# Triangular inverse in the delta-rule mixer: 64x64 diagonal blocks throughout, or 32x32 blocks for the first four levels

## What is computed

```
m = jnp.where(strict, jnp.einsum("bhnid,bhnjd->bhnij", k_beta, k) * decay, 0.0)
a_mat = jnp.eye(CHUNK, dtype=q.dtype) + m
u = lax.linalg.triangular_solve(a_mat, v_beta, left_side=True, lower=True)
w = lax.linalg.triangular_solve(a_mat, k_beta * jnp.exp(g)[..., None], left_side=True, lower=True)
```

## Time and profile before

| | |
|---|---|
| median of 3 runs | 1297.12 us (1296.31 to 1297.67) |
| the profiled execution, its own time | 1297.02 us |
| its span | 1295.2 us |
| PE busy | 1258.4 us, 97% of the span |
| VectorE busy | 994.9 us, 77% |
| ScalarE busy | 685.0 us, 53% |
| GpSimd busy | 53.7 us, 4% |
| chain that ended last | PE 73%, VectorE 6%, DMA 2% |

### The profile page before, as it was taken

How to read it: one execution, slowest core, us unless ns; L and a number is a source line. 1 busy time by engine, 2 the same in 40 slices (tenths; PEclk the granted TensorE clock), 3 DMA queues, 4 the chain that set the end, 5 groups by cost and what they waited for, 6 DMA issues and landing times.

```text
span 1295.2 us, 29136 instructions
## 1 busy us (share of the span) xinstructions
PE 1258.4 (97%) x10579; PEld 1210.5 (93%) x10579; DVE 994.9 (77%) x1817; ACT 685.0 (53%) x1116; POOL 53.7 (4%) x93
## 2 busy tenths in 40 slices
PE   9999998999999999999999999999999999999997
PEld 8989898999999899999998899998899999999986
DVE  6897748998878898998877787775566668777654
ACT  6865435655543544665553555554365565645541
POOL 0002000000001000000000000000000000000000
PEclk9999999999999999999999999999999999999999
DMA  7550123588888588388875366665455335666651
GB/s 269 160 150 2 52 82 115 199 301 278 294 281 278 200 291 270 113 305 278 276 252 167 98 198 184 186 197 192 135 179 180 125 106 178 189 184 179 227 177 34
DMA packets 64778, 244.74 MB, mean 189 GB/s; under 512 B 7200, under 2 KB 8512, under 8 KB 64704
## 3 DMA queue, kind: packets, MB, share of 16 engines
q1 hardware_dynamic: 54048, 204.77, 48.7%
q0 software_dynamic: 10656, 38.93, 9.5%
HBM read 242.63 MB, written 1.05 MB: 188 GB/s over the span
## 4 chain that ended last, share of the span: by engine, by line
PE 73%; DVE 6%; DMA 2%; issue 1%; ACT 1%; DVEq 0%; POOLq 0%; ACTq 0%
PE ps L1778 17%; PE ps L1779 17%; PE ps L1780 16%; PE ps L2137 9%; PE ps L2138 5%; DMA ring<-in_ada_w 2%; DVE wlo L410 1%; PE ps L1793 1%; PE ps L1799 1%; PE ps L1794 1%; DVE ring L1298 1%; PE ps L2282 1%; PE ps L2284 1%; PE ps L2283 1%; DVE xb L1423 1%
## 5 line engine op out<-in xcount | busy, mean ns | idle before, releaser
L1778 PE MATMUL ps<-hhi,whi 128*128 128x258 f32 (+4 forms) x1952 | 557.6, 286 | 5.0 <-DVE hlo L1038 1.9
L1779 PE MATMUL ps<-hlo,whi 128*128 128x258 f32 (+4 forms) x1952 | 553.8, 284 | 0.0
L1780 PE MATMUL ps<-hhi,wlo 128*128 128x258 f32 (+4 forms) x1952 | 553.3, 283 | 0.0
L403 ACT ACTIVATE whi<-raw 128x1024 fp32r<-128x1024 f32 (+1 forms) x360 | 399.9, 1113 | 285.2 <-PE ps L1780 166.3
L410 DVE TENSOR_TENSOR wlo<-raw,whi 128x1024 fp32r<-128x1024 f32 (+1 forms) x360 | 463.4, 1292 | 84.8 <-ACT whi L403 82.7
L1778 PEld LDWEIGHTS ps<-hhi,whi 128*128 128x128 f32 x1952 | 369.4, 189 | 7.5 <-issue 4.6
L1780 PEld LDWEIGHTS ps<-hhi,wlo 128*128 128x128 f32 x1952 | 370.5, 190 | 0.0
L1779 PEld LDWEIGHTS ps<-hlo,whi 128*128 128x128 f32 x1952 | 370.2, 190 | 0.3
L2137 PE MATMUL ps<-aboth,whi 128*128 128x512 f32 x528 | 185.6, 396 | 0.0
L2138 PE MATMUL ps<-aboth,wlo 128*128 128x256 f32 x528 | 147.9, 280 | 0.0
L2137 PEld LDWEIGHTS ps<-aboth,whi 128*128 128x128 f32 x528 | 99.3, 188 | 23.2
(11 more groups left out here) (416 smaller groups left out, 1557.4 us busy)
## 6 DMA issues: line engine op xcount, KB each, us to landing
raw<-in_w_up SPq DMA_DIRECT2D x176, 512.0 KB, 3.9
raw<-in_w_down SPq DMA_DIRECT2D x64, 704.0 KB, 4.7
ring<-in_ada_w POOLq DMA_DIRECT2D x72, 512.0 KB, 5.3
raw<-in_w_mix SPq DMA_DIRECT2D x48, 512.0 KB, 3.6
raw<-in_w_a_in SPq DMA_DIRECT2D x32, 512.0 KB, 3.6
raw<-in_w_b_cx SPq DMA_DIRECT2D x16, 512.0 KB, 5.2
raw<-in_w_a_out SPq DMA_DIRECT2D x8, 512.0 KB, 3.6
raw<-in_w_b_gate SPq DMA_DIRECT2D x8, 512.0 KB, 4.7
```

The source lines that it names most:

```text
L403: nc.scalar.activation(whi[:, s, 0:blocks * P], raw[:, s, 0:blocks * P], ACT.Copy).then_inc(hi_split, 1)
L1778: nc.tensor.matmul(out, whi[:, s, w], rhi(k0 + k), start=first and k == 0, stop=False)
L1779: nc.tensor.matmul(out, whi[:, s, w], rlo(k0 + k), start=False, stop=False)
L1780: ins = nc.tensor.matmul(out, wlo[:, s, w], rhi(k0 + k), start=False, stop=last and k == blocks - 1)
```

## The change

Levels 0 to 4 (blocks of up to 32) are kept one step finer: the four 32x32 diagonal blocks of each 128x128 block stand under each other in the first 32 columns (`SMALL`). The products x and y of levels 1 to 4, the turns of levels 0 to 3 and the meta values are now four multiplications of 32x32 by 32x32 per block, one for each quarter of rows, where there were two of 64x64. The reads behind them cover 128 partitions by 32 columns per block (128 for a group). `first_inverse` has four multiplications of 32 partitions in place of two of 64. At the end of level 4 `add_y` has two operations: it adds into `ex`, then spreads `ex` to the 64 columns of `gu` with a mask that puts each quarter into its half and zeroes elsewhere. From the turn of level 4 on all is as before. `STEPS` and the banks stay as they are, and the constants in `cm` change in content, not in number.

```diff
--- before.py
+++ after.py
@@ -34,6 +34,9 @@
 TOP, HALF = LEVELS - 1, P // 2
 LOW, HIGH = slice(0, HALF), slice(HALF, P)
 HALVES = (LOW, HIGH)
+FINE, QUARTER = 4, P // 4
+QUARTERS = [slice(q * QUARTER, (q + 1) * QUARTER) for q in range(4)]
+SMALL = QUARTERS[0]
 
 
 STEPS = [
@@ -132,7 +135,7 @@
 
 
 C_IDENT, C_MEAN, C_ONES, C_CAUSAL, C_CAUSAL_META, C_SAME_META, C_LEVEL = range(7)
-C_PAIR, C_ONE, C_DIAG = C_LEVEL, C_LEVEL + 1, C_LEVEL + TOP
+C_PAIR, C_ONE, C_SPREAD, C_DIAG = C_LEVEL, C_LEVEL + 1, C_LEVEL + 2, C_LEVEL + TOP
 N_CONST = C_LEVEL + LEVELS
 
 
@@ -383,6 +386,10 @@
 
             return ps[7] if i >= ONE_BANK_TURNS and (i - ONE_BANK_TURNS) % 2 == 0 else ps[3]
 
+        def quarters_at(bank, n):
+
+            return bank[:, 0:n * QUARTER].rearrange("p (b t) -> p b t", t=QUARTER)
+
         def halves_at(bank, n, part=slice(0, P)):
 
             return bank[part, 0:n * HALF].rearrange("p (b t) -> p b t", t=HALF)
@@ -604,6 +611,9 @@
                 if l == 0:
                     act.wait_ge(qg_ready, OPENS_AT[g] + 1)
                 act.wait_ge(mm_turn, i + 1)
+                if l < FINE:
+                    nc.scalar.activation(gt[:, b0:b0 + n, SMALL], quarters_at(turn_bank(i), n), ACT.Copy).then_inc(tu_ready, 1)
+                    return
                 part = LOW if l == TOP - 1 else slice(0, P)
                 nc.scalar.activation(gt[part, b0:b0 + n, LOW], halves_at(turn_bank(i), n, part), ACT.Copy).then_inc(tu_ready, 1)
 
@@ -1190,10 +1200,10 @@
 
                 b0, n = GROUPS[g]
                 dve.wait_ge(m_ready, OPENS_AT[g] + 1)
-                for half in HALVES:
-                    last = nc.vector.tensor_tensor(gu[half, b0:b0 + n, LOW], bn[half, b0:b0 + n, half], bcast(cm[half, C_PAIR, LOW], n), ALU.mult)
+                for q in QUARTERS:
+                    last = nc.vector.tensor_tensor(gu[q, b0:b0 + n, SMALL], bn[q, b0:b0 + n, q], bcast(cm[q, C_PAIR, SMALL], n), ALU.mult)
                 step(last)
-                nc.vector.tensor_tensor(gu[:, b0:b0 + n, LOW], gu[:, b0:b0 + n, LOW], bcast(cm[:, C_DIAG, LOW], n), ALU.add).then_inc(gu0_ready, 1)
+                nc.vector.tensor_tensor(gu[:, b0:b0 + n, SMALL], gu[:, b0:b0 + n, SMALL], bcast(cm[:, C_DIAG, SMALL], n), ALU.add).then_inc(gu0_ready, 1)
 
             def mask_x(m):
                 (l, g), j = m, MERGE_AT[m]
@@ -1203,6 +1213,9 @@
                     dve.wait_ge(ca_ready, OPENS_AT[g] + 1)
                 if l == TOP:
                     nc.vector.tensor_scalar(ex[HIGH, b0:b0 + n, LOW], halves_at(ps[j % 2], n, HIGH), -1.0, None, ALU.mult).then_inc(x_ready, 1)
+                elif l <= FINE:
+                    nc.vector.tensor_tensor(ex[:, b0:b0 + n, SMALL], quarters_at(ps[j % 2], n),
+                                            bcast(cm[:, C_LEVEL + l, SMALL], n), ALU.mult).then_inc(x_ready, 1)
                 else:
                     nc.vector.tensor_tensor(ex[:, b0:b0 + n, LOW], halves_at(ps[j % 2], n),
                                             bcast(cm[:, C_LEVEL + l, LOW], n), ALU.mult).then_inc(x_ready, 1)
@@ -1213,6 +1226,14 @@
                 dve.wait_ge(mm_y, j + 1)
                 if l == TOP:
                     nc.vector.tensor_copy(gu[LOW, b0:b0 + n, HIGH], halves_at(y_bank(j), n, LOW)).then_inc(gu_ready, 1)
+                elif l < FINE:
+                    nc.vector.tensor_tensor(gu[:, b0:b0 + n, SMALL], gu[:, b0:b0 + n, SMALL], quarters_at(y_bank(j), n), ALU.add).then_inc(gu_ready, 1)
+                elif l == FINE:
+                    step(nc.vector.tensor_tensor(ex[:, b0:b0 + n, SMALL], gu[:, b0:b0 + n, SMALL], quarters_at(y_bank(j), n), ALU.add))
+                    nc.vector.tensor_tensor(gu[:, b0:b0 + n, LOW].rearrange("p b (c t) -> p b c t", t=QUARTER),
+                                            ex[:, b0:b0 + n, SMALL].unsqueeze(2).to_broadcast([P, n, 2, QUARTER]),
+                                            bcast(cm[:, C_SPREAD, HIGH], n).rearrange("p b (c t) -> p b c t", t=QUARTER),
+                                            ALU.mult).then_inc(gu_ready, 1)
                 else:
                     nc.vector.tensor_tensor(gu[:, b0:b0 + n, LOW], gu[:, b0:b0 + n, LOW],
                                             halves_at(y_bank(j), n), ALU.add).then_inc(gu_ready, 1)
@@ -1951,9 +1972,13 @@
                     to = slice((b - b0) * HALF, (b - b0 + 1) * HALF)
                     if l == TOP:
                         last = nc.tensor.matmul(ps[j % 2][HIGH, to], bn[LOW, b, HIGH], gt[LOW, b, LOW], start=True, stop=True)
-                    else:
+                    elif l > FINE:
                         for half in HALVES:
                             last = nc.tensor.matmul(ps[j % 2][half, to], bn[half, b, half], gt[half, b, LOW], start=True, stop=True)
+                    else:
+                        to = QUARTERS[b - b0]
+                        for q in QUARTERS:
+                            last = nc.tensor.matmul(ps[j % 2][q, to], bn[q, b, q], gt[q, b, SMALL], start=True, stop=True)
                 last.then_inc(mm_x, 1)
 
             def y_mm(m):
@@ -1971,9 +1996,13 @@
                     to = slice((b - b0) * HALF, (b - b0 + 1) * HALF)
                     if l == TOP:
                         last = nc.tensor.matmul(y_bank(j)[LOW, to], ex[HIGH, b, LOW], gu[HIGH, b, LOW], start=True, stop=True)
-                    else:
+                    elif l > FINE:
                         for half in HALVES:
                             last = nc.tensor.matmul(y_bank(j)[half, to], ex[half, b, LOW], gu[half, b, LOW], start=True, stop=True)
+                    else:
+                        to = QUARTERS[b - b0]
+                        for q in QUARTERS:
+                            last = nc.tensor.matmul(y_bank(j)[q, to], ex[q, b, SMALL], gu[q, b, SMALL], start=True, stop=True)
                 last.then_inc(mm_y, 1)
 
             def turn(m):
@@ -1994,6 +2023,11 @@
                     if l == TOP - 1:
                         last = nc.tensor.transpose(turn_bank(i)[LOW, to], gu[LOW, b, LOW], ident[LOW, LOW])
                         continue
+                    if l < FINE:
+                        to = QUARTERS[b - b0]
+                        for q in QUARTERS:
+                            last = nc.tensor.matmul(turn_bank(i)[q, to], gu[q, b, SMALL], ident[q, q], start=True, stop=True)
+                        continue
                     for half in HALVES:
                         last = nc.tensor.matmul(turn_bank(i)[half, to], gu[half, b, LOW], ident[half, half], start=True, stop=True)
                 last.then_inc(mm_turn, 1)
@@ -2002,8 +2036,8 @@
 
                 pe.wait_ge(gu_ready, MERGE_AT[3, 4] + 1)
                 pe.wait_ge(tr_read, ROWS.index((1, 4)) + 1)
-                for half in HALVES:
-                    last = nc.tensor.matmul(ps[4][half, 0:P], gu[half, MB, LOW], v_b(MB)[half, :], start=True, stop=True)
+                for q in QUARTERS:
+                    last = nc.tensor.matmul(ps[4][q, 0:P], gu[q, MB, SMALL], v_b(MB)[q, :], start=True, stop=True)
                 last.then_inc(mm_v0, 1)
 
             def meta_s0():
@@ -2441,11 +2475,16 @@
     i, j = np.arange(P)[:, None], np.arange(P)[None, :]
     same = i // META == j // META
     out = [i == j, np.full((P, P), 1.0 / D), np.ones((P, P)), i <= j, same & (i <= j), same]
-    i, j = i % HALF, np.where(j < HALF, j, P)
+    p, full = i, j
+    i, j = p % QUARTER, np.where(full < QUARTER, full, P)
     out.append(-1.0 * ((i >> 1 == j >> 1) & (i < j)))
     for l in range(1, TOP):
+        if l > FINE:
+            i, j = p % HALF, np.where(full < HALF, full, P)
         out.append(-1.0 * ((i >> (l + 1) == j >> (l + 1)) & (i >> l & 1 == 1) & (j >> l & 1 == 0)))
     out[C_ONE][:, HALF + 31] = 1.0
+    out[C_SPREAD] = np.where(full < HALF, out[C_SPREAD], (full - HALF) // QUARTER == p // QUARTER % 2)
+    i, j = p % QUARTER, np.where(full < QUARTER, full, P)
     out.append((i == j) | (np.arange(P)[:, None] % AB == np.arange(P)[None, :] - HALF))
     return np.ascontiguousarray(np.stack(out, 1).astype(np.float32))
```

## The result

| | before | after |
|---|---|---|
| median | 1296.71 us (4 runs) | 1312.31 us (4 runs, 1310.53 to 1313.27) |
| ratio | | 1.0116, 95% interval 1.0104 to 1.0129 |
| span of the profiled execution | 1295.2 us | 1308.7 us |
| q8, packets of instructions | 52 | 58 |
| y of step 26 starts | 146.81 us | 160.93 us |

The change makes the kernel 15.6 us slower, where 6 us faster was predicted. The loss lies where the change is. In the profiled executions PE's last branch ahead of the changed code is 0.75 us later than before (59.06 for 58.31 us), the y of step 7 is 0.44 us late (116.44 for 116.00), the y of step 26 is 14.1 us late (160.93 for 146.81), and PE's starts from there to 175 us are all 13.8 to 14.1 us late.

The account below looks back on a forecast made before the run. PE, busy for 97% of the span, was taken to bound the kernel; 5.3 us from steps 7 to 25 plus 0.7 us before them, off 1297.02, gave 1291.0 us, range 1286.8 to 1299.0.

Parts of the forecast that it names:

- What is late next: Steps 7 to 25: taking the longer of PE and VectorE per step gives 25.5 us, so 5.3 us saved.
- Before and behind them: Outside steps 7 to 25: 0.7 us saved before them, nothing from step 26; PE's weights no obstacle.
- the 0.7 us that the sum had ahead of step 7: Turns of groups 0 and 1, and group 3's turn, x and y, save 0.7 us together (0 to 1.2).
- the round of 33 ns: Fine products on PE: four 32x32 tiles side by side take 33 ns per round, a full group 264 ns for 467.
- VectorE's reads: mask_x and add_y on 128 elements take 0.29 us for 0.42, 3.3 us less VectorE work in steps 7 to 25.
- the spread: add_y at level 4: a spread of 256 elements takes 0.42 us; with add and wait, +0.3 us four times.
- the changes of shape: PE from step 20 on: 7 more changes between tile shapes at some 0.1 us each, +0.7 us (0 to 1.4).
- Rate of starts: Rival, fine products: PE starts come no faster than 27.3 ns on average, a group 0.87 us, kernel 1316 us; chance 0.11.
- The clock falls: Rival, fine stage: thinner PE work lowers the granted clock for some 15 us, +7 us against -6, 1298 us; chance 0.05.
- A round doesn't shrink: Rival, fine products: a group stays at 0.44 to 0.47 us, no change, 1297.8 us; chance 0.14.

Follow-up runs that it names:

- e9: The kernel before with x of levels 1 to 4 alone as four products of 32x32 tiles per block, on the old storage: 1301.77 us, ratio 1.0033.
- e2: The changed kernel with an idle 128x512 product on PE at the start of each of steps 9 to 22: 1312.40 us, ratio 1.0123.
- e11: The kernel before with twin products in the idle quadrants for x alone in steps 9 to 22, 376 instructions more: 1299.69 us, ratio 1.0019.
- e8: The kernel before, each fine 64x64 product in steps 9 to 22 twinned in an idle quadrant, results unread, 1112 instructions more: 1311.05 us, ratio 1.0104.

## Why the prediction was wrong

**The step that failed is "What is late next"**, and with it the claim in "Before and behind them" that PE's inputs are no obstacle, which looked at weights alone. With PE's array work shortened I asked only VectorE's turn: "I go through the steps and take the longer of PE and VectorE in each", 25.5 us. What was late next was PE's own instruction stream. Steps 7 to 25 took 44.5 us (116.44 to 160.93) where 25.5 were predicted. Twelve transfers begin between 116.3 and 157.7 us, 11 distances in 41.4 us, 3.8 us each. The number of blocks times their distance, not the longer of two engines, makes the stage. Of the 0.7 us that the sum had ahead of step 7 the profiled executions show 0.3 (0.75 us late at the last branch, 0.44 at the y of step 7). What held: the round of 33 ns (groups of 0.27 to 0.33 us), VectorE's reads (0.27 to 0.29 us), the spread (0.42), the changes of shape (0.1 us, in e9).

**It was to be had from the profile of before.** The page lists 52 q8 packets and the DMA view shows each; in the fine stage they stand 4 to 5.5 us apart, 256 instructions in each. 64 instructions in 0.264 us ask for a block every 1.1 us while groups follow each other, and with the row transposes the blocks of the changed kernel start all their records within 1.8 to 2.9 us from 121.95 to 139.89 us. No transfer of before was closer than 3.9 us to its neighbour in that stage, so nothing bore out such a rate; that was worth a rival with a large chance.

**The rival "Rate of starts"** had the right side and nearly the right size (1316; 1312.3 came). Its mechanism was wrong: the starts are not held apart, 32 of them lie in 0.27 us; whole blocks are late. Its numbers are of another kind, too. Its threshold of 14.6 ns is per MATMUL start, the supply's 13.3 to 14.8 ns is per instruction, and half of the instructions are weight loads. Its price, 27.3 ns per start, is 13.7 ns per instruction and so the pace of the supply; but it was read from rows where 58 ns and 109 ns rounds set the distance, so that it fits is luck as far as any run shows. Its chance of 0.11 was too small, because I took a few fast starts in the earlier trace rows as evidence against it, and a few records say nothing of a sustained rate. By the Trainium skill, TensorE: Matmul & The Clock Gate, section "Wait — 56ns, not 53.3ns?", read over all tiles, a start comes no closer than 25 ns; the trace after disagrees, at about 8 ns over four tiles, and only its time (1313) came near, by chance.

**"The clock falls"** happened (0.50 for some 20 us) and costs little or nothing in the changed kernel, by e2 and the 0.43 us of a group at half clock; that rival had it cost 7 us. **"A round doesn't shrink"** is refuted. **Not shown:** why the next transfer begins only some 1.3 us after PE has entered a block, and why 2.2 to 2.7 us pass from there to the first of its instructions, when its packet takes about 1; how much is held ahead (the traces fit one block, no run measures it); whether weight loads delay a block (the distances of 5.0, 5.6 and 5.5 us in the changed kernel, e9 and e11 lie beside them, and there the transfer begins 2.7 to 3.1 us after PE has entered the block; no experiment took the loads away). That the stops are late instructions is inferred from the count of 256, their places in the program, the q8 transfers and e8 together; the profile has no wait that names them.

## What to carry to other kernels

In straight-line code, give PE's instructions a price beside the array's: count those that PE would run through in 3.4 to 4 us, and if they are over 256, expect the time to be the number of blocks times that, whatever the array does. No run here measures the other engines' supply. A float32 product costs four instructions, so splitting a product into smaller tiles saves only as long as a block still lasts. When PE shows "issue" in the middle of a group, count the records between the stops before looking for a semaphore: the same number each time points at the supply.

## What the runs showed of the hardware

- PE's instruction blocks of 256: in the changed kernel from 116 to 138 us 3.4 to 3.8 us apart (13.3 to 14.8 ns per instruction), 3.9 us on the mean in e8. PE's first record of a block stands 2.2 to 2.7 us behind the begin of a transfer at each of 16 stops, and the next transfer mostly begins 1.2 to 1.5 us later.
- Float32 rounds over all tiles: 33 ns with 32x32 weights and 32 moving columns, 58 ns with 64x64 weights for 64 and for 32 moving. At half clock a group of 8 rounds of the former took 0.43 us in place of 0.27.
- Four 64x64 quadrants run at once: with the twins of e8 a round is still 58 ns.
- VectorE's transpose of a 128x256 float32 tile takes 0.45 us, little more than an addition (0.42).
